# Recurrent stage of a two-block layer: doubling products on four array quarters, the second head's rows swapped, key lengths inverted token by token

## The reference, cut to what matters

```
kk = (k * k_k).reshape(bsz, t, heads, 64)
kk = kk / max(sqrt(sum(kk * kk, axis=-1)), 1e-12)          # key lengths, per token and head
def step(state, inp):                                      # 512 steps, 2 directions, 8 heads
    sa = einsum('dbhij,dbhj->dbhi', state, a_t)            # a = -kk
    state = state * w_t + sa * b_t + v_t * k_t             # b = kk * rate
    return state, einsum('dbhij,dbhj->dbhi', state, r_t)
```

## Time and profile before

| | us |
|---|---|
| median of the runs | 2017.88 |
| profiled execution | 2017.0 |
| its span | 2015.2 |
| PE busy (share of the span) | 1819.2 (90%) |
| DVE busy | 1027.5 (51%) |
| ACT busy | 689.7 (34%) |
| recurrent stage (`rwkv_block`), about | 1159 to 1468 |
| of it the eight units | 1186 to 1426 |

### The profile page before, as it was taken

The page is one execution under the profiler, slowest core; times in us unless marked ns, Lnnn a source line. Parts: engine busy times, 40 slices in busy tenths (PEclk is TensorE's granted clock), DMA queues, the critical chain, the costliest instruction groups (busy, mean ns, idle before and its releaser), DMA issues. The chain is left out here.

```text
span 2015.2 us, 37871 instructions
## 1 busy us (share of the span) xinstructions
PE 1819.2 (90%) x16732; PEld 1563.5 (78%) x16732; DVE 1027.5 (51%) x1586; ACT 689.7 (34%) x1121; POOL 88.5 (4%) x115
## 2 busy tenths in 40 slices
PE   5998889888999999898999769999679899999978
PEld 5898768888989989686777558888558688788867
DVE  4246564455645646447554366575655534343444
ACT  3242234533433423333332254444143323232322
POOL 6000000010000000100000000000001100000020
PEclk8999879988999999989999989999889899999999
DMA  5211130111222222222122000000052122222211
GB/s 156 84 64 43 53 105 1 65 42 63 88 100 84 105 84 90 101 78 74 52 84 89 37 23 4 4 4 9 3 219 84 64 104 87 101 92 97 97 71 63
DMA packets 29258, 144.53 MB, mean 72 GB/s; under 512 B 6315, under 2 KB 9659, under 8 KB 14508
## 3 DMA queue, kind: packets, MB, share of 16 engines
q1 hardware_dynamic: 25116, 134.10, 18.4%
q0 software_dynamic: 3696, 7.35, 1.3%
q10 hardware_dynamic: 288, 0.73, 0.1%
HBM read 134.82 MB, written 8.91 MB: 71 GB/s over the span
## 5 line engine op out<-in xcount | busy, mean ns | idle before, releaser
L228 DVE TENSOR_TENSOR w_w_lo<-w_w_raw,w_w_hi 128x2048 fp32r<-128x2048 f32 x67 | 153.5, 2292 | 182.5 <-ACT w_w_hi L215 182.2
L240 PE MATMUL f_bank<-u_hi,w_w_hi 128*128 128x258 f32 x704 | 203.3, 289 | 12.3 <-DVE w_w_lo L228 6.1
L241 PE MATMUL f_bank<-u_hi,w_w_lo 128*128 128x258 f32 x704 | 202.2, 287 | 0.0
L242 PE MATMUL f_bank<-u_lo,w_w_hi 128*128 128x258 f32 x704 | 200.7, 285 | 0.0
L240 PE MATMUL g_bank<-g_u_hi,g_w_hi 128*128 128x512 f32 x384 | 152.6, 397 | 17.5 <-DVE g_u_lo L2714 14.1
L241 PE MATMUL g_bank<-g_u_hi,g_w_lo 128*128 128x512 f32 x384 | 151.1, 394 | 0.0
L242 PE MATMUL g_bank<-g_u_lo,g_w_hi 128*128 128x512 f32 x384 | 150.9, 393 | 0.0
L240 PE MATMUL g_bank<-g_y_hi,g_w_hi 128*128 128x512 f32 x336 | 133.0, 396 | 18.9 <-DVE g_w_lo L228 12.0
L240 PEld LDWEIGHTS f_bank<-u_hi,w_w_hi 128*128 128x128 f32 x704 | 135.1, 192 | 13.7 <-issue 6.4
L215 ACT ACTIVATE g_w_hi<-g_w_raw 128x2048 fp32r<-128x2048 f32 x45 | 85.9, 1909 | 173.9 <-PE g_bank L242 171.3
L215 ACT ACTIVATE w_w_hi<-w_w_raw 128x2048 fp32r<-128x2048 f32 x67 | 127.6, 1904 | 32.0 <-PE f_bank L242 32.0
(11 more groups left out here) (457 smaller groups left out, 4156.2 us busy)
## 6 DMA issues: line engine op xcount, KB each, us to landing
g_w_raw<-in_w_ff SPq DMA_DIRECT2D x32, 1024.0 KB, 4.7
w_w_raw<-in_w_in SPq DMA_DIRECT2D x30, 1024.0 KB, 4.8
w_w_raw<-in_w_ffn_in SPq DMA_DIRECT2D x22, 1024.0 KB, 4.8
w_w_raw<-in_w_ffn_out SPq DMA_DIRECT2D x12, 1024.0 KB, 4.8
w_w_raw<-in_w_o SPq DMA_DIRECT2D x4, 1024.0 KB, 5.0
gate_pre<-rw_t POOLq DMA_DIRECT2D x16, 256.0 KB, 2.3
g_w_raw<-in_w_up SPq DMA_DIRECT2D x4, 1024.0 KB, 9.0
g_branch<-gate_pre SPq DMA_DIRECT2D x4, 1024.0 KB, 11.2
```

The source lines that it names most:

```text
L228: nc.vector.tensor_tensor(R.lo[:, r, 0:size], R.raw[:, r, 0:size], R.hi[:, r, 0:size].bitcast(F32), ALU.subtract).then_inc(R.split, 1)
L240: nc.tensor.matmul(out, w_hi, u_hi, start=start, stop=False)
L241: nc.tensor.matmul(out, w_lo, u_hi, start=False, stop=False)
L242: return nc.tensor.matmul(out, w_hi, u_lo, start=False, stop=stop)
```

## The change

Head 1's `z` and `x_t` are kept with the two chunk halves swapped (half 0 in partitions 64 to 127). The z product, P, `keys_values` and the `wu` product so use all four pairs of row and column halves, both heads in one group of 16. Pt reads and writes the swapped rows for both, and stays on two quarters at a time. ACT drains z, and DVE copies x and x_t, with one instruction for both heads in place of two. For the first level of `x_t` head 1 is needed with its halves swapped, so `attention` has 8 matmuls more in its first group. `turn_keys` replaces the transposes of a: 16 matmuls of 64x64 that put head 1's halves swapped, placed behind the z product of level 5. `keys_values` moves to level 2. `decay_sums`, `directed_rate`, `scale_bonus` and `scale_reads` are pieces of DVE's preparation with places of their own.

The key lengths are summed with two columns of `head_ones`, tokens in the partition: 128x32 for all head pairs. One root, one maximum and one reciprocal are taken of those; PE turns them to 8x512 and spreads them over 128 partitions with a selector, and `unit_keys` reads the spread lengths from PSUM.

The diff, cut to its core:

```diff
+        swap = lambda hh, half: hp(half ^ hh)
+        QUADS = ((0, 0), (0, 1), (1, 0), (1, 1))
...
+            def turn_keys(u):
+                fi, d = unit(u)
+                pe.wait_ge(tt_done, 4 * u + 1)
+                for hh in range(2):
+                    out = side(turn_at(u) + hh)
+                    for t in range(NB):
+                        for half in range(2):
+                            tk = slice(P * t + CH * half, P * t + CH * half + CH)
+                            last = nc.tensor.matmul(out[swap(hh, half), t * HD:t * HD + HD], a_s[hp(hh), d, tk],
+                                                    C("ident")[hp(hh), hh * HD:hh * HD + HD], start=True, stop=True)
+                    last.then_inc(side_done, 1)
...
+                products(b_s, a_s, 4, 0, hh, half, own)
+                products(b_s, a_s, 4, W, (1, 1), (0, 1), (hp(1), hp(0))).then_inc(a_done, 1)
...
+                pe.wait_ge(a_read, 6 * u + 2)
+                products(k_s, r_s, 2, W, hh, half, own).then_inc(a_done, 1)
...
-                    block_products(lambda half, t: bank[hp(half), 4 + hh, t * CH:t * CH + CH],
-                                   lambda half, t: ab_t[hp(half), hh, t, :], lambda half, t: x[hp(half), hh, t, :]).then_inc(z_done, 1)
...
+                block_products(lambda hh, half, t: bank[swap(hh, half), 4 + hh, t * CH:t * CH + CH],
+                               lambda hh, half, t: ab_t[hp(half), hh, t, :], lambda hh, half, t: x[hp(half), hh, t, :]).then_inc(z_done, 1)
+            def update(u, k):
+                pe.wait_ge(z_read, NX * u + k)
+                if k == 1:
+                    pe.wait_ge(a_read, 6 * (u + 1))
+                else:
+                    pe.wait_ge(xt_done, NX * u + k - 1)
+                if k < NX:
+                    block_products(lambda hh, half, t: bank[hp(half), 2 + hh, t * CH:t * CH + CH],
+                                   lambda hh, half, t: x_t[swap(hh, half), hh, t, :],
+                                   lambda hh, half, t: z[swap(hh, half), hh, t, :]).then_inc(p_done, 1)
+                for h in range(2):
+                    last = block_products(lambda hh, half, t: bank[swap(hh, half), hh, t * CH:t * CH + CH],
+                                          lambda hh, half, t: z[swap(hh, half), hh, t, :],
+                                          lambda hh, half, t: x_t[swap(hh, half), hh, t, :], ((h, 0), (h, 1)))
+                last.then_inc(pt_done, 1)
...
+                pe.wait_ge(xt_done, NX * (u + 1))
+                block_products(lambda hh, half, t: bank[hp(half), 2 + hh, t * P:t * P + P],
+                               lambda hh, half, t: x_t[swap(hh, half), hh, t, :],
+                               lambda hh, half, t: wr[swap(hh, half), d, hh, t, :]).then_inc(wu_done, 1)
...
                 for k in range(1, LEVELS):
-                    double(u, k)
-                    if k == 1:
+                    level_products(u, k)
+                    if k == 2:
                         keys_values(u)
+                    if k == NX and u + 1 < NU:
+                        turn_keys(u + 1)
+                    update(u, k)
...
+                    act.wait_ge(z_done, NX * u + k)
+                    nc.scalar.activation(changed_in(z, k, u % 2), changed_out(4, k, u % 2), ACT.Copy).then_inc(z_read, 1)
+                    if k == 2:
                         keys_values(u)
-                    if k == 2 and u + 1 < NU:
-                        decays(u + 1)
+                        if u + 1 < NU:
+                            decays(u + 1)
```

More of the change, by code:

```diff
@@ L2066, in attention @@
                 pe.wait_ge(tt_done, 4 * (u + 1))
[L2067 to L2075, removed]
-                    for t in range(NB):
[L2077 to L2081, removed]
@@ L2083, in block_products, with products @@
-            def block_products(out, left, right):
+                if u == 0:
+                    pe.wait_ge(kk_done, RW_FI)
+                def products(left, right, b, at, hh, half, out):
+                    for t in range(NB):
+                        for h, f, o in zip(hh, half, out):
+                            tk = slice(P * t + CH * f, P * t + CH * f + CH)
+                            last = nc.tensor.matmul(bank[o, b + h, at + t * CH:at + t * CH + CH], left[hp(h), d, tk],
+                                                    right[hp(h), d, tk], start=True, stop=True)
+                    return last
@@ L2085, in block_products @@
+                products(b_s, r_s, 0, 0, hh, half, own).then_inc(a_done, 1)
+                products(k_s, a_s, 0, W, hh, half, own).then_inc(a_done, 1)
+                pe.wait_ge(a_read, 6 * u + 2)
+                products(k_s, r_s, 2, W, hh, half, own).then_inc(a_done, 1)
+            def block_products(out, left, right, quads=QUADS):
                 for t in range(NB):
-                    for half in range(2):
-                        last = nc.tensor.matmul(out(half, t), left(half, t), right(half, t), start=True, stop=True)
@@ L2165, in late @@
                 last.then_inc(d_done, 1)
-            for fi in range(RW_FI):
-                pe.wait_ge(sqk, fi + 1)
-                nc.tensor.matmul(bank[:, fi, :], C("head_ones"), bz[:, fi % 2, :], start=True, stop=True).then_inc(ksum, 1)
             pe.wait_ge(in_loaded, 32)
@@ L2374, in masked @@
                     return nc.vector.tensor_tensor(dst[:], two(b, at), both(mask(name)), ALU.mult)
-                def first_level(dst, b, side):
-                    return nc.vector.copy_predicated(dst[:], both(first[:, side, :]), two(b, 0))
                 dve.wait_ge(x_init, 2 * (u + 1))
@@ new lines, in _ @@
+                    nc.vector.copy_predicated(changed_in(x_t, k, 1 - u % 2), level(1 - u % 2, k), changed_out(0, k, 1 - u % 2)).then_inc(xt_done, 1)
+                    if more and k == 1:
+                        sums(u + 1)
+                    elif more and k == 2:
+                        directed_rate(u + 1)
+                    elif more and k == 3:
+                        directed(u + 1)
+                        scale_bonus(u + 1)
+                    elif more and k == 4:
+                        scale(u + 1)
```

251 lines of the change are left out of this document (135 added, 116 removed).

## The result

The changed kernel takes 2022.06 us (median of 20 runs, 2017.04 to 2027.34), the kernel before 2017.99 us beside it (20 runs). The ratio is 1.0020, 95% interval 1.0010 to 1.0029: slower by 4.1 us, where 11.3 us less were forecast.

A forecast was written before the change was run, and what follows sets the result against it. PE was taken as the limit, DVE close behind. Gains of 8.9 us (units 0 to 6), 2.4 us (unit 7) and 0 (start) made 11.3 us off 2017.0: 2005.7, or 2006.5 us as median; range 1993 to 2019.

The forecast's parts named there:

- the late part: In each unit, from the wu group to the products with wu: 5.7 us before, to fall by 0.84 us.
- The mechanism: Skill rule that weight loads overlap matmuls only across row groups; would make `turn_keys` 1.87 us instead of 0.93.
- Gotcha 1: PSUM Pressure: Slower rival: quarters sharing a PSUM bank serialize in z, P and wu groups; 30 us more, 2036 us; chance 0.07.
- units 0, 2, 4, 6: Even units: 1.4 us less in each, from the levels (0.6 us) and the late part (0.84 us); 5.6 us together.
- unit 7: Last unit, which prepares nothing: levels from 2.94 to 2.56 us apiece, 2.4 us less with last level and wu.
- The zero: At the start, `scale_reads` 2 to 3 us later cancels PE's turning 2 to 3 us shorter; bounds 3 us either way.
- no gain: Rival: column pairs serialize, or DVE's merged copies reach their upper bound with a start 3 us later; 2016 us, chance 0.16.
- the walk: One unit followed step by step from the start of `attention`, pricing groups, drains and copies; wu at 19.4 against 20.0 us.
- 3.6 us that no semaphore explains: PE's waits inside the groups of line 2079 in the kernel before, across all eight units, listed among PE's waits.
- what might come out better: Larger-gain rival: stalls without a semaphore and copies improve and the start gains 3 us; up to 24 us, 1993, chance 0.06.
- denser instruction issue: Slower rival: something unpriced in the start or in instructions issued more densely; no size given, chance 0.05 for both together.
- The full clock kept: Sign that the forecast is right: PE keeps its full 2.4 GHz clock (1.00 granted), as in the units before.

The follow-up runs named there:

- E2: The kernel before with only the new token-wise key lengths, without the array change: ratio 1.0003 to the kernel before, +0.6 us.
- E1: The changed kernel with the key lengths of before, so the array change only: ratio 1.0047 to the kernel before, +9.5 us.
- E5: The changed kernel plus three wide unread products behind z of level 3 in seven units: ratio 1.0027 to the kernel before, +5.4 us.
- E10: The changed kernel with exponentials behind level 3 and the first head's `turn_keys` as four full transposes: ratio 1.0003 to the kernel before, +0.6 us.

## Why the prediction was wrong

The mechanism on the array was read rightly, and most prices with it: groups of 16 on four quarters 0.47 to 0.52 us apart, `turn_keys` 0.81 us in the units, the update of level 3 released by ScalarE behind the exponentials, the late part 4.73 us from wu (4.87 forecast), PE busy 31.7 us less in the units (some 35 forecast). Neither rule of the Trainium skill that was weighed against them held here: the case of TensorE: Matmul & The Clock Gate, Part 3, "The mechanism", was priced at 1.87 us for `turn_keys`, that of TensorEngine Tiling (Array Packing), "Gotcha 1: PSUM Pressure", at 0.93 us for a z group; the rows read 0.81 and 0.49. But 2022.1 us lies above the whole range of 1993 to 2019. By the terms of its sum:

| us | forecast | measured (means of three) |
|---|---|---|
| start | 0 | +5.2 |
| units 0, 2, 4, 6 | -5.6 | 0.0 |
| units 1, 3, 5 | -3.3 | -0.9 |
| unit 7 | -2.4 | 0.0 |

The three executions behind each mean differ by up to 1.6 us before and 4.1 us after in the row of the even units, and by less in the others. E2, in one profile, has what the key lengths do by themselves: they take 6.2 us out of the units. So the array change, which was to bring the gain, adds some 5 us there (240.5 against 235.3; E1 has 6.5 over before). The number failed at these steps.

**The start, taken as 0, was +5.2 us**, outside the bounds of 3 either way. The zero was 2 to 3 us more on VectorE against 2 to 3 less on PE. `scale_reads` ended 4.8 us later and not 2 to 3 (25.7 us after the stage's start, 20.9 before), and from its first turning to `attention` PE took 6.4 us, where it had taken 6.0. The spreading was counted as one link of the chain and not as PE time. It takes PE 7.2 us at half clock, and `turn_keys` begins only behind it, 25.2 us after the stage's start, where PE's turning of before began at 20.9 (1180.15 in the earlier trace rows). E1 and E2 show that the whole of it is the key lengths.

**Copies of short runs.** The copies of levels 0 and 1 measure 0.72 to 0.78 us; against 0.58 that is some 0.7 us for the four of them. It is this that sets unit 0 back: P of level 3 at 12.34 against 11.7, wu at 20.0 against 19.4, no earlier than before. In five levels I had it as a range of 0.75 us a unit under "no gain"; it is four copies, all ahead of the exponentials. VectorE's last mask, rk_t, holds back the first update (5.04 against 4.6). Of the 1.4 us forecast for unit 0, 0.65 us went here. Another 0.7 us went at its end, where the part behind the late one got longer by that much around the wait for issue at 1222.74. What is left is 0.2 us: 30.5 against 30.7.

**Products had no price of their own.** I counted PE's time by groups and left instructions out. The change adds 324 executed products to the eight units (16 in each, and 28 for `turn_keys` in seven), which at 20 to 29 ns are an estimated 6 to 9 us, and lets groups of 0.47 us follow one another, which uses up a block in half the time that the next needs to come. The row was there: the waits for issue, "3.6 us that no semaphore explains". I put it only under what might come out better, and gave "denser instruction issue" part of 0.05.

**"The full clock kept" was wrong** in 4, 5 and 2 of the eight units in three executions. After the long wait of level 3, weight loads of a group that take 0.56 us take 0.94:

```profile
1266.06 0.56 PEld L2111 LDWEIGHTS r_bank<-r_z,r_x_t 64*64 64x64 f32 x32 [2.59 <-ACT r_z L2344]
...
1269.34 0.94 PEld L2111 LDWEIGHTS r_bank<-r_z,r_x_t 64*64 64x64 f32 x32 [0.70 <-ACT r_z L2344]
```

What it cost is not shown. Unit 5 of the kernel after takes 29.40 us with a mean of 0.94 and 29.47 and 29.12 us with 1.00, but unit 0 takes 31.26 and 31.25 with 0.95 and 30.49 with 1.00, and unit 6 takes 30.57 and 30.48 with 0.94 and 29.11 with 1.00. Against a large share of the loss speaks E5: its wide products fill most of the wait, all its eight units are at 1.00, and it is no faster than the kernel after.

**The gain of the key lengths was put inside the walk.** It is a term of its own, 6 us in the units, and it is what keeps the array change from showing as E1's loss of 9.5.

**One unit stood for all.** "A unit with an even number lasts 30.7 us" is true of unit 0. Units 2 and 4 took 32.4 and 32.1 us before, with five waits for issue between them, where unit 0 has none, and no walk was made of them. In unit 7 the levels run at 2.60 us apiece as forecast (2.56), but from z of level 5 to wu it takes 2.9 to 3.5 us, where it took 2.3 before: PE now waits 0.64 us there for the copy of both heads' x_t, and had no wait before. The first update, held by the last mask, starts 6.6 us into the unit, where P started at 5.5. Nothing of the 2.4 us is left.

What remains unexplained: E10's loss, what the spells of half clock cost, and the units' own spread of 4 us between executions of one kernel.

## What to carry to other kernels

Where small products follow one another, count the executed instructions as well as PE's time: here 128 products with their weight loads need 3.5 to 3.75 us to come, so running a long stream of them on four quarters at 14.7 ns each gives nothing beyond that pace, and merging products that share weights does. When two chains become one, look for what stands between its steps on the other engines (here the exponentials and the reciprocals): the second chain was the cover. And small work put into an engine's idle gap has to be priced at the clock that the gap leaves it.

## What was not expected of the hardware

- PE's instructions come in packets of 256 (16 KB), one in 3.47 or 3.75 us when nothing else waits, though the queue's share of the 16 DMA engines is 1.9% meanwhile. A wait for them shows as "issue", and ends 1.2 to 1.7 us after a packet has landed.
- The stage's starting point lies anywhere from 1157.5 to 1163.2 us in executions whose code ahead of it is the same.
- A full 128x128 weight load with two columns takes 218 ns a piece on PE at half clock (6.99 us for 32), more than the 8 executed products of 512 columns that did the same sums before (1160.36 to 1166.38 us, 6.02, at a granted 0.61).
